# Slot-0 modulation columns in two groups of 512 channels instead of four of 256, in the first stage of a hybrid trunk kernel

## What is computed

```
sc, sc_ctx = silu(c), silu(c_ctx)
m  = (sc     @ ada_w[0] + ada_b[0]).reshape(B, 9, 1, D)    # shift, scale, gate for 3 slots
mc = (sc_ctx @ ada_w[0] + ada_b[0])
a  = h * (1 + m[:, 1]) + m[:, 0]                           # slot 0: input of the first FFN
h  = post_norm(ALPHA * h + 0.5 * m[:, 2] * ffn(a))
# filter (needed by the first mixer only): three small layers with sin, a decay window, rfft
h1 = sin(fr1 * (feats @ w1 + b1)); h2 = sin(fr2 * (h1 @ w2 + b2)); taps = (h2 @ w3 + b3) * window
k_hat = rfft(taps) * rsqrt(sum(taps ** 2))
```

## Time and profile before

| | |
|---|---|
| timed runs, median | 1700.55 us |
| profiled execution, span | 1695.6 us |
| TensorE busy | 1662.0 us, 98% |
| VectorE busy | 1177.9 us, 69% |
| ScalarE busy | 709.6 us, 42% |
| mean granted TensorE clock | 0.992 |
| first matmul of the regular loop (L2086) starts | 60.96 us |
| TensorE busy from 0 to 60.9 us | 50.20 us |
| HBM traffic from 0 to 60.9 us | 322 GB/s |

### The profile page before, as it was taken

How to read it: one execution, slowest core, us unless ns; L and a number is a source line. 1 busy time by engine, 2 the same in 40 slices (tenths; PEclk the granted TensorE clock), 3 DMA queues, 4 the chain that set the end, 5 groups by cost and what they waited for, 6 DMA issues and landing times. The chain is left out here.

```text
span 1695.6 us, 23534 instructions
## 1 busy us (share of the span) xinstructions
PE 1662.0 (98%) x9103; PEld 1399.8 (83%) x9103; DVE 1177.9 (69%) x1852; ACT 709.6 (42%) x1157; POOL 72.8 (4%) x62
## 2 busy tenths in 40 slices
PE   7999999999999999999999999999999999989997
PEld 5788888889877889888888898888888888888886
DVE  5577958887586866778633476879466787777767
ACT  4542232234645436422222237322322267666454
POOL 1000000001000020000000020000000110100001
PEclk9999999999999999999999999999999999999998
DMA  9665546632321231655322233554466342145653
GB/s 319 239 210 171 165 150 218 212 98 93 105 84 54 75 125 55 207 180 160 119 100 83 84 133 127 196 180 144 159 218 206 94 137 88 63 146 169 208 173 112
DMA packets 86949, 248.37 MB, mean 146 GB/s; under 512 B 8884, under 2 KB 24981, under 8 KB 86838
## 3 DMA queue, kind: packets, MB, share of 16 engines
q1 hardware_dynamic: 86360, 245.98, 44.1%
q0 software_dynamic: 256, 0.46, 0.1%
q10 hardware_dynamic: 222, 0.43, 0.1%
HBM read 245.79 MB, written 1.05 MB: 146 GB/s over the span
## 5 line engine op out<-in xcount | busy, mean ns | idle before, releaser
L1275 DVE TENSOR_TENSOR w_lo<-raw,w_hi 128x1024 fp32r<-128x1024 f32 (+2 forms) x337 | 380.6, 1129 | 155.0 <-ACT w_hi L831 148.3
L2086 PE MATMUL bank<-a_both,w_hi 128*128 128x512 f32 (+1 forms) x1200 | 462.8, 386 | 2.3 <-DVE w_lo L1275 1.4
L2088 PE MATMUL bank<-a_both,w_hi 128*128 128x512 f32 (+1 forms) x1200 | 460.8, 384 | 0.0
L2087 PE MATMUL bank<-a_both,w_lo 128*128 128x512 f32 (+1 forms) x1200 | 460.7, 384 | 0.0
L831 ACT CAST w_hi<-raw 128x1024 fp32r<-128x1024 f32 (+2 forms) x337 | 320.3, 957 | 161.2 <-DMA raw<-in_dram 147.6
L2086 PEld LDWEIGHTS bank<-a_both,w_hi 128*128 128x128 f32 x1200 | 225.9, 188 | 48.6 <-issue 2.3
L2088 PEld LDWEIGHTS bank<-a_both,w_hi 128*128 128x128 f32 x1200 | 225.8, 188 | 44.8
L2087 PEld LDWEIGHTS bank<-a_both,w_lo 128*128 128x128 f32 x1200 | 226.0, 188 | 43.9
L1293 DVE SCALAR_TENSOR_TENSOR acc<-ada,scol,acc 128x1024 f32<-128x1024 f32 x189 | 234.9, 1280 | 9.5 <-DMA ada<-in_dram 7.7
L2086 PE MATMUL bank<-h_both,w_hi 128*128 128x512 f32 (+1 forms) x473 | 183.6, 388 | 0.8 <-DVE w_lo L1275 0.8
L944 ACT CAST h_both<-tmp_b 128x512 fp32r<-128x512 f32 (+1 forms) x88 | 50.0, 569 | 320.0 <-DVE tmp_b L1528 292.6
(11 more groups left out here) (336 smaller groups left out, 2242.9 us busy)
## 6 DMA issues: line engine op xcount, KB each, us to landing
raw<-in_dram SPq DMA_DIRECT2D x229, 512.0 KB, 4.1
ada<-in_dram SPq DMA_DIRECT2D x120, 512.0 KB, 4.0
raw<-in_dram SPq DMA_DIRECT2D x64, 384.0 KB, 3.1
raw<-in_dram SPq DMA_DIRECT2D x64, 320.0 KB, 3.0
first<-in_dram SPq DMA_DIRECT2D x32, 256.0 KB, 6.5
first<-in_dram SPq DMA_DIRECT2D x8, 512.0 KB, 8.6
hz<-in_dram SPq DMA_DIRECT2D x4, 512.0 KB, 7.6
out_dram<-hz SPq DMA_DIRECT2D x8, 128.0 KB, 1.7
```

Source lines behind the costliest of these rows:

```text
L1275: V.tensor_tensor(lo_of(n)[:, 0:cols], raw[:, n % RING, 0:cols], hi_of(n)[:, 0:cols].bitcast(F32), ALU.subtract).then_inc(s["lo_ready"], 1)
L2086: pe.matmul(dst, w_at(0), x_at(0), start=first, stop=False, skip_group_check=shared)
L2087: pe.matmul(dst, w_at(1), x_at(0), start=False, stop=False, skip_group_check=shared)
L2088: return pe.matmul(dst, w_at(0), x_at(1), start=False, stop=last, skip_group_check=shared)
```

## The change

The columns come in two groups of 512 channels, eight entries each, one DMA an entry with rows of 2 KB instead of 1 KB. A `first_sum` is four MATMULs of 256 columns instead of eight of 128. Turning a group takes two small products. SyncE issues group 0, quarter 0, x 0, quarter 1, x 1, then group 1, quarter 2, x 2, quarter 3, x 3. All filter loads, the window (four DMAs) and the DFT table (two) move to ScalarE's queue. The second pass of `apply_x` becomes `middle` on VectorE. The order of all four engines is new, and TensorE gets 22 products of ones with ones (`warm`) between the first sums and behind the first turn; their result is not used. The gate's eight entries are summed with the same wide form and turned in one step.

```diff
-GATE_Q = 4 * PAIRS
+GATE_Q = 2 * KC
+WIDE = 2 * P
 ...
-                    g, q = divmod(d, PAIRS)
-                    for kk in range(2):
-                        src = ada_d[0, 0, 2 * q + kk].rearrange("p (s c) -> p s c", s=3)
-                        sp.dma_start(room.rearrange("p (k s c) -> p k s c", k=2, s=2)[:, kk],
-                                     src[:, 0:2, g * 2 * P:(g + 1) * 2 * P]).then_inc(first_in[d % QUEUE], 16)
+                    g, k = divmod(d, KC)
+                    src = ada_d[0, 0, k].rearrange("p (s c) -> p s c", s=3)[:, 0:2, g * 4 * P:(g + 1) * 4 * P]
+                    sp.dma_start(room.rearrange("p (s c) -> p s c", s=2), src).then_inc(first_in[d % QUEUE], 16)
 ...
-            for d in range(PAIRS):
-                load_first(d)
-            load_x(0)
-            load_quarter(0)
+            for g in range(2):
+                for d in range(KC * g, KC * (g + 1)):
+                    load_first(d)
+                for x in (2 * g, 2 * g + 1):
+                    load_quarter(x)
+                    load_x(x)
             pos[0] = 4
 ...
+            for t, d in ((feats, feats_d), (fw1, fw1_d), (fw2, fw2_d), (fw3, fw3_d)):
+                act.dma_start(t[:], d).then_inc(s["filter_in"], 16)
+            def load_tables():
 ...
+                for b in range(2):
+                    rows = slice(b * GCH, (b + 1) * GCH)
+                    act.dma_start(window[rows, 0:2, :], by_token[:, :, b, :]).then_inc(s["window_in"], 16)
+                    act.dma_start(window[rows, 2, :], by_token[:, 0, 2 + b, :]).then_inc(s["window_in"], 16)
+                for b in range(2):
+                    act.dma_start(dft0[b * GCH:(b + 1) * GCH], turns[:, :, b, :, 0:P]).then_inc(s["dft0_in"], 16)
 ...
+                def middle(c):
 ...
+                    for w in range(2):
+                        cols = slice(w * SEQ, (w + 1) * SEQ)
+                        ins = V.tensor_scalar(tmp_b[:, c % 2, cols], hz[:, c, cols], acol[:, 0, w, 0, c:c + 1],
+                                              acol[:, 0, w, 1, c:c + 1], ALU.mult, ALU.add)
+                    ins.then_inc(s["am_ready"], 1)
 ...
+                for j in range(4):
+                    ins = pe.matmul(bank[7][32 * j:32 * (j + 1), g % 2 * WIDE:(g % 2 + 1) * WIDE], scolp[:, k, :],
+                                    first[:, d % QUEUE, j * WIDE:(j + 1) * WIDE], start=(k == 0), stop=(k == KC - 1),
+                                    skip_group_check=True)
 ...
+                def warm(n):
+
+                    for _ in range(n):
+                        pe.matmul(bank[3][:, 0:P], ones[:], ones[:], start=True, stop=True)
```

TensorE's new order, from the wait for the silu on:

```diff
+                warm(2)
+                for d in range(3):
+                    first_sum(d)
+                    warm(2)
                 pe.wait_ge(s["filter_sin"], 1)
                 pe.matmul(fbank(1)[0:FHID, 0:SEQ], fw2[:], fh[0:FHID, 0, :], start=True, stop=True)\
                     .then_inc(s["filter_h"], 1)
+                for d in range(3, 6):
+                    first_sum(d)
+                    warm(2)
                 tap(0)
                 tap(1)
+                first_sum(6)
+                tap(2)
+                tap(3)
+                first_sum(7)
+                turn_sums(0)
+                warm(8)
                 first_chunk(0)
                 first_chunk(1)
+                first_sum(8)
+                first_sum(9)
+                first_chunk(2)
+                for d in range(10, 13):
+                    first_sum(d)
                 spectrum(0)
+                spectrum(1)
+                for d in range(13, 16):
+                    first_sum(d)
+                chunk_high(3)
                 turn_sums(1)
+                chunk_low(3)
+                first_chunk(4)
+                first_chunk(5)
                 spectrum(2)
                 spectrum(3)
                 first_chunk(6)
                 last_chunk()
```

More of the change, by code:

```diff
@@ L880, in keep @@
                 if n == 0:
+                    act.wait_ge(s["am_ready"], c + 1)
                     A.activation(hz[:, c, :], hz[:, c, :], ACT.Copy, scale=ALPHA).then_inc(s["ah_ready"], 1)
@@ L1641, in take_taps @@
                         .then_inc(s["taps_read"], 1)
-                take_cols(0)
-                quarter_lo(0)
-                lower(0)
-                lower(1)
-                dve.wait_ge(s["window_in"], 96)
-                for i in range(4):
-                    take_taps(i)
                 def rotated(kind):
@@ L1661, in mixed @@
                                         (ALU.add, ALU.subtract)[kind]).then_inc(s["taps_mixed"], 1)
-                dve.wait_ge(s["taps_read"], 4)
-                rotated(0)
-                mixed(0)
-                take_sums(1)
-                rotated(1)
-                take_cols(1)
-                mixed(1)
                 def mirrored(kind):
@@ L1677, in mirrored @@
                         .then_inc(s["spectrum_read"], 1)
-                quarter_lo(1)
-                lower(2)
-                lower(3)
-                mirrored(0)
-                take_sums(2)
-                take_cols(2)
-                quarter_lo(2)
-                lower(4)
-                lower(5)
-                mirrored(1)
-                take_sums(3)
-                quarter_lo(3)
-                take_cols(3)
-                split_to(5)
-                lower(6)
+                dve.wait_ge(s["window_in"], 64)
+                take_taps(0)
+                take_taps(1)
+                rotated(0)
+                rotated(1)
+                take_taps(2)
+                take_taps(3)
+                take_sums(0)
+                take_cols(0)
+                quarter_lo(0)
+                for c in (0, 1):
+                    middle(c)
+                    lower(c)
+                quarter_lo(1)
+                for c in (2, 3):
+                    middle(c)
+                    lower(c)
+                dve.wait_ge(s["taps_read"], 4)
+                mixed(0)
+                mixed(1)
+                take_sums(1)
+                take_cols(1)
+                quarter_lo(2)
+                for c in (4, 5):
+                    middle(c)
+                    lower(c)
+                mirrored(0)
+                quarter_lo(3)
+                for c in (6, 7):
+                    middle(c)
+                    lower(c)
+                split_to(5)
+                mirrored(1)
                 split_to(RING - 1)
-                lower(7)
             def filter_scale():
@@ L2147, in turn_sums @@
                 pe.wait_ge(s["first_read"], g + 1)
-                pe.matmul(bank[6][:, 8 * g:8 * g + 8], sums0[:, g % 2, :],
-                          ident[:].rearrange("p (a r) -> p a r", r=32)[:, :, 0:2], start=True, stop=True)\
-                    .then_inc(s["first_turned"], 1)
+                for h in range(2):
+                    ins = pe.matmul(bank[6][:, 16 * g + 8 * h:16 * g + 8 * h + 8], sums0[:, g % 2, h * P:(h + 1) * P],
+                                    ident[:].rearrange("p (a r) -> p a r", r=32)[:, :, 0:2], start=True, stop=True)
+                ins.then_inc(s["first_turned"], 1)
             def norm_sums(m, w):
```

141 lines of the change are left out of this document (44 added, 97 removed).

## The result

The changed kernel takes 1702.78 us (median of 20 runs, 1698.44 to 1704.24) against 1699.30 for the kernel before beside it (20 runs, 1695.39 to 1701.18). The ratio is 1.0019, 95% interval 1.0013 to 1.0025: 3.2 us slower, where 1695.05 had been predicted. The profiled execution has a span of 1699.9 us against 1695.6. Every timed execution is counted in the ratios of this document, but one of E14 that took 3735.35 us.

What follows compares the result with a forecast made beforehand. TensorE, 98% busy, was taken as the bound, fed by first-stage transfers: 24.3 + 21.8 + 3.7 + 3.8 + 0.3 + 1.6 = 55.5 us against 60.96, so 1700.55 - 5.5 = 1695.05 us; 8-in-10 range 1691.8 to 1700.5.

Steps and rivals of the forecast that it cites:

- ScalarE's queue: the sine slips by 0.5 to 2.5 us and costs nothing: Start of first stage: nine more loads on ScalarE delay the first sine from 8.66 us, hidden behind waits for entries.
- Group 0 complete at 20.6: First stage transfers: group 0's last entry lands at 20.6 us, from 21.8 less 1.0 and 0.7, plus 0.5.
- The interleaving for which I added 0.5 us: Group 0's transfers: entries taking turns with the tables were charged 0.5 us in its completion time.
- Chunk 0 at 24.3: First stage on TensorE: chunk 0 starts at 24.3 us, 7.3 us later than before (17.02).
- TensorE from there, 31.2 us: Chunk 0 to regular loop: chunks 21.8, sums 3.7, spectra 3.8, turn 0.3, waits 1.6 us, ending at 55.5.
- the step that called VectorE's work hidden: First stage chunks: with `middle`, VectorE needs 4.5 us for two chunks, under TensorE's 5.46, so hidden.
- the clock rival: TensorE stays at lower clock into chunk 0: 6.7 us lost, 1701.8 us; chance shared in cases of 0.17, 0.11, 0.07.
- Group 1's landing at 38.0: First stage transfers: group 1's last entry lands at 38.0 us, bounds 36.4 and 39.4.
- The bound of 36.4 with 401 GB/s: Early bound for group 1's landing, if both groups' entries move at 401 GB/s; moves the loop by -0.4 us.
- The rival named a landing at 43.5 us: Late transfers: group 1 landing after 43.5 us gains nothing; 47 us gives 1704.1; chance shared in cases of 0.11 and 0.07.
- The products of ones lie in the waits for entries: First sums on TensorE: fourteen `warm` products hide in waits for entries; without waits they would cost 3.3 us.
- the no-gain case: Whole kernel at 1700 to 1704 us, through no gain or the clock or transfer rival; chance 0.11.

Runs made afterwards that it cites:

- E14: E15 with two products of ones behind each of sums 12 to 15; 1695.20 us, ratio 0.9979 to the kernel before.
- E1: Changed kernel with its four filter loads at the head of SyncE's queue, tables left in place; ratio 1.0010 to the kernel before.
- E11: Changed kernel with SyncE's first entry held until the four filter loads have landed; run once, 1697.66 us, only its profile read.
- E3: Kernel before the change with its three small filter loads moved to ScalarE's queue; ratio 1.0007 to the kernel before.
- E13: E12 with the four filter loads on ScalarE's queue again; median 1700.87 us, ratio 1.0011 to the kernel before.
- E5: E1 with window and DFT tables on SyncE's queue behind group 0, quarter 0 and x 0; ratio 1.0032 to the kernel before.
- E8: E6 with the window and DFT tables early on ScalarE's queue; ratio 1.0028 to the kernel before.
- E6: E5 reordered: sums 6, 7 ahead of taps, taps 0, 1 replacing `warm(8)`, taps 2, 3 behind chunk 1 and sums 8, 9; ratio 1.0005.
- E4: Changed kernel with `middle` back on ScalarE; ratio 1.0004 to the kernel before.
- E2: Changed kernel without its 22 products of ones; ratio 1.0007 to the kernel before.
- E12: E9 with taps 2 and 3 ahead of entry 8, ScalarE's squares and GpSimd's additions moved to 50 us; median 1698.18 us, ratio 0.9994.
- E15: E12 with ScalarE's squares of the taps back at 32 to 39 us; 1695.38 us against 1698.92, ratio 0.9979.
- E10: Changed kernel with the filter loads ahead of the parameters on ScalarE's queue; run once, 1703.19 us, only its profile read.
- E9: E6 with chunks 0 to 3 back to back, then sums 8 to 15 around taps 2 and 3; tables behind `x1`; ratio 0.9996.
- E7: E6 without its fourteen products of ones; ratio 1.0001 to the kernel before.

## Why the prediction was wrong

*ScalarE's queue: the sine slips by 0.5 to 2.5 us and costs nothing.* This step failed, and twice. The first product slipped by 5.7 us. I had charged ScalarE for issuing, which was right (the tables were issued by 9 us), and not the landing: the loads' bytes share the engines with eight entries of 512 KB that SyncE had issued from 0.74 us on. The first sine stood at 14.36 us instead of 9.2 to 11.2. Timeline of the changed kernel, ScalarE's queue:

```profile
1.93 1.83 ACTq L789 DMA_DIRECT2D fw<-in_dram  x3
```

The weights were issued by 3.8 us and used at 10.70. SyncE at the head of its queue had them by 5.83 (E1), ScalarE with SyncE held by 7.08 (E11). And the cover I named, sums 3 to 5 that wait for their entries until 17 us anyway, left out that all the sums are queued behind it, and that TensorE needs its rounds of sum and ones, at up to 2.2 us each at the lower step. The price was 1 to 3 us in the old kernel (E3) and 2.3 to 2.7 in E13.

*Group 0 complete at 20.6.* The rate was about right (313 GB/s in 6 to 24 us for the 323 assumed: 5.1 MB take 0.5 us more), the order in which the bytes arrive was not. The two queues (q1 SyncE's, q10 ScalarE's) in two windows of the changed kernel, 4 to 7 us, with the filter weights in flight, and 15 to 17 us, with the tables; packets, MB, share:

```profile
q1 hardware_dynamic: 551, 1.06, 97.2%
q10 hardware_dynamic: 133, 0.06, 7.2%
...
q1 hardware_dynamic: 182, 0.35, 65.1%
q10 hardware_dynamic: 176, 0.21, 41.5%
```

While the tables move the two queues get nearly the same number of packets (182 and 176 here, 272 and 272 in 17 to 19 us), and ScalarE's smaller ones take the entries' turns: entries come 2.1 us apart (E1), and without the tables no sum waits at 1.2 us apart (E5). While the filter weights are in flight it is not so: ScalarE's queue gets 133 packets of 684. That SyncE's entries held them is shown by E11; why they got so small a share is not. The interleaving for which I added 0.5 us cost chunk 0 up to 5.8, clock included (E8 against E6). The Trainium skill (DMA: Bandwidth & Descriptors, "Issuing engines are not separate DMA queues") says that DMAs of several engines interleave on the same 16 engines and that a second issuer saves only issue time. The trace agrees: 182 packets against 176, and with the second issuer 313 GB/s in 6 to 24 us against 323. Weighed beforehand, it would have been the rival that was missing.

*Chunk 0 at 24.3.* 30.99, 6.7 us late. Removing either cause gave 0.9 us (E1) or made it worse (E5): each wait was covered by the next, and the four taps ahead of sums 6 and 7 tied the sums to the window's arrival. With filter loads, tables and order all put right it was 22.70 (E6). At the loop E6 has 2.3 us of the 3.1 back. So filter loads, tables and order together are shown for most of the 3.2 us, and `middle` for 1.2 us of the profile (E4), a share that cannot be told apart from theirs in the times.

*TensorE from there, 31.2 us.* 64.07 - 30.99 = 33.1. The waits come to 1.7 us (0.64 at `chunk_low(0)`, 0.18 ahead of chunk 3, 0.49 ahead of chunk 4, 0.41 ahead of the loop) where 1.6 had been forecast, but in other places: the entries cost none of their 0.4, and the step that called VectorE's work hidden failed. It weighed VectorE's 4.5 us for two chunks against TensorE's 5.46, and had 0.3 for the start of the chunks and nothing for the end, where TensorE has nothing queued to cover the work: without `middle` both waits are gone (E4, 1.2 us in all). At the start something came on top: one of quarter 0's four subtractions took 1.24 us instead of 0.43, beside GpSimd additions that ran from 27.88 to 30.57, so the four took 2.62, in E4 too, where it cost no wait. `middle` itself took 0.37 for each half of a chunk, as forecast (0.35), which makes two per chunk: 0.73. The chunks are the larger miss: chunk 5, in full flow, takes 56.29 - 53.55 = 2.74, as forecast, but those that follow sums, a turn or a wait take about 3.0, and all eight some 23.3 instead of 21.8. The sums took 3.9 for 3.7. Steps of 0.23 in chunk 0 from its second matmul on were right, so the clock rival did not come about; without ones it does (E2).

*Group 1's landing at 38.0.* The bound of 36.4 with 401 GB/s was mis-summed: 40.4 - 1.0 - 2 x (4.19/0.358 - 4.19/0.401) is 36.9; nothing hung on it. In E12, where TensorE waits for it, the last entry is summed from 39.89: 1.9 us late and 0.5 beyond the bound of 39.4. It never mattered in the changed kernel, whose last sum ends at 46.4. The rival named a landing at 43.5 us, which is a last sum ending at 44.1, as the point from which nothing is gained. 46.4 is 2.3 beyond it, and 17.7 us of work followed instead of 16.9; together that is the 3.1 us. The arithmetic of that rival held, its cause did not: not the rate, but the order of arrival and the queue on TensorE.

*The products of ones lie in the waits for entries.* There were no such waits in the changed kernel, since TensorE started 5.7 us late. The prediction named this case (3.3 us), and counted from the first product to the last sum of group 0 it is 3.3: 27.18 - 10.70 against 24.89 - 11.74 in E2. On chunk 0 2.1 us of it are seen, and the clock gives them back.

*The range* ended at 1700.5 because none of the cases had the first product late; the cases that reached beyond it (0.07 slower, part of the no-gain case) rested on the clock and the rate. Of the forecast gain of 5.5 us E15 has 3.8 at the loop (57.12 against 60.96 before) and 3.5 in the times. It is not shown that the wide groups bring it: E15 also moves loads and reorders all engines, and no run gives the four narrow groups the same order.

## What to carry to other kernels

Moving loads to a second queue added no bandwidth here (313 GB/s against 323 in 6 to 24 us): it gave the loads of the first queue a competitor, and the small loads came late themselves. So put what the first instruction needs at the head of the deep queue, and what is needed late behind everything else. Where an engine's queue strings several waits together, an edit that removes one shows little; move the late consumer behind the early ones first (here taps behind sums), then price each load. When adding up a stage, charge a load until it lands, beside everything issued by then, not until it is issued. And work on an engine that is hidden in full flow is still paid at the ends of the stage, where nothing is queued to cover it (`middle`, 1.2 us).

## What was unexpected in the hardware

- Small loads beside a deep queue land late: 57 KB and 260 KB issued by 3.8 us on ScalarE's queue were used at 10.70, 10.02 when issued first (E10), 7.08 with SyncE's queue empty (E11), 5.83 at the head of SyncE's (E1).
- VectorE instructions were stretched while GpSimd added, in the changed kernel too (a subtraction of 128x256 in quarter 0, 1.24 us against 0.43): two `tensor_scalar` of 128x256 float32 took 2.84 us (E6) and 2.83 (E12) against 0.73, four additions of 128x512 4.55 and 4.57 (E9, E15) against 2.50. By the Trainium skill (SBUF — State Buffer, "SBUF: two separate sides") the two engines share a port pair, and when VectorE's instruction runs in a two-port mode, or has two inputs in SBUF while GpSimd reads there, whichever starts first holds the pair for its whole instruction and the other blocks. The trace agrees with the blocking: a pair of 0.73 us lasts 2.84 beside two additions of 2.72 together. In which mode VectorE's instructions ran no run shows.
- Leaving the products of ones out made chunk 0 run at the 1.2 GHz level in both orders (E2 all of it, E7 its first half), and yet no loss of time could be measured: with them the changed kernel is at 1.0019 (1.0013 to 1.0025), without them at 1.0007 (0.9997 to 1.0018), and E6 and E7 overlap too. Nor do the waits alone tell the clock: E12 and E15 have similar ones ahead of the spectra and differ in level.
